# Sliding-window attention in a fused two-layer kernel: norm and softmax work moved between engines, first token tile run to its end first

## The reference, cut to what matters

```python
def mixer_c(h, w_in, q_norm, k_norm, sinks, rel_bias, w_out):
    proj = h @ w_in                                   # 1024 -> 1024 (q) + 256 (k) + 256 (v)
    q, k, v = jnp.split(proj, [SW_HEADS * SW_DIM, (SW_HEADS + SW_KV_HEADS) * SW_DIM], axis=-1)
    q = rmsnorm_2(q.reshape(B, S, SW_HEADS, SW_DIM), q_norm)       # 16 heads of 64
    k = rmsnorm_2(k.reshape(B, S, SW_KV_HEADS, SW_DIM), k_norm)    # 4 heads of 64
    ...
    o = sliding_window_attention(q, k, v, sinks, rel_bias)
    return o.reshape(B, S, C_OUT) @ w_out
# inside, per block of 128 queries against its own and the previous 128 keys:
    logits = jnp.einsum('bqhgd,bkhd->bhgqk', qn, kn) * scale + bias
    m = jnp.maximum(jnp.max(logits, axis=-1, keepdims=True), sink)
    e = jnp.exp(logits - m)
    w = e / (jnp.sum(e, axis=-1, keepdims=True) + jnp.exp(sink - m))
    return jnp.einsum('bhgqk,bkhd->bqhgd', w, vn)
```

## Time and profile before

| | us |
|---|---|
| median of three runs | 1542.4 (1539.7 to 1542.81) |
| span of the profiled execution, first to last instruction | 1536.3 |
| what lies around the span, median less span | 6.1 |
| TensorE busy | 1381.1 |
| VectorE busy | 1029.5 |
| ScalarE busy | 710.5 |
| GpSimd busy | 568.9 |

### The profile page before, as it was taken

How to read it: one execution, slowest core, us unless ns; L and a number is a source line. 1 busy time by engine, 2 the same in 40 slices (tenths; PEclk the granted TensorE clock), 3 DMA queues, 4 the chain that set the end, 5 groups by cost and what they waited for, 6 DMA issues and landing times.

```text
span 1536.3 us, 18265 instructions
## 1 busy us (share of the span) xinstructions
PE 1381.1 (90%) x6001; PEld 969.0 (63%) x6001; DVE 1029.5 (67%) x1917; ACT 710.5 (46%) x1377; POOL 568.9 (37%) x541
## 2 busy tenths in 40 slices
PE   7999998778777887777779999999999999999998
PEld 6887963323333333333336878788888778888887
DVE  4885787666666666666655548659863686498734
ACT  5545453222333332233324463477645655776534
POOL 3040454333333333333344422055433512364414
PEclk9999999998998999999899999999999999999999
DMA  9295699999999999999998510567665443476650
GB/s 315 91 179 189 247 385 422 421 421 422 422 421 422 420 423 422 421 422 422 422 421 312 192 48 13 165 184 203 191 216 194 158 140 92 134 207 195 214 188 28
DMA packets 180739, 414.99 MB, mean 270 GB/s; under 512 B 9178, under 2 KB 113218, under 8 KB 148418
## 3 DMA queue, kind: packets, MB, share of 16 engines
q0 software_dynamic: 37440, 268.45, 42.1%
q1 hardware_dynamic: 143090, 145.66, 30.9%
q10 hardware_dynamic: 144, 0.04, 0.0%
HBM read 409.93 MB, written 4.19 MB: 270 GB/s over the span
## 4 chain that ended last, share of the span: by engine, by line
PE 52%; DMA 23%; DVE 9%; ACT 6%; POOL 5%; issue 4%; ACTq 0%; POOLq 0%; DVEq 0%
DMA expert_rows<-in_peer_uv,route_idx 13%; PE ps L2522 10%; DMA work_b<-in_peer_uv,route_idx 9%; PE ps L2347 8%; PE ps L2063 8%; PE ps L2065 8%; PE ps L2064 8%; PE ps L2523 5%; POOL weights_lo L588 2%; POOL expert_rows L637 2%; ACT weights_hi L433 2%; DVE weights_lo L440 2%; PE ps L2028 1%; DVE expert_rows L1645 1%; POOL ple_proj_lo L588 1%
## 5 line engine op out<-in xcount | busy, mean ns | idle before, releaser
L1645 DVE CUSTOM_DVE_ANT_0 expert_rows<-expert_rows,ps 128x1024 f32<-128x1024 f32 x180 | 219.4, 1220 | 133.9 <-DMA expert_rows<-in_peer_uv,route_idx 132.0
L2347 PE MATMUL ps<-expert_rows,proj 128*128 128x512 f32 x512 | 248.6, 644 | 63.5 <-ACT proj L952 63.5
L637 POOL DMA_INDIRECT expert_rows<-in_peer_uv,route_idx x191 | 184.5, 966 | 288.9 <-PE ps L2347 218.9
L588 POOL TENSOR_TENSOR weights_lo<-weights_raw,weights_hi 128x512 fp32r<-128x512 f32 x116 | 153.4, 1356 | 352.2 <-ACT weights_hi L433 310.3
L433 ACT CAST weights_hi<-weights_raw 128x2048 fp32r<-128x2048 f32 x98 | 185.5, 1917 | 106.3 <-PE ps L2065 82.6
L2347 PEld LDWEIGHTS ps<-expert_rows,proj 128*128 128x128 f32 x512 | 102.9, 206 | 208.4 <-issue 122.5
L2522 PE MATMUL ps<-x_normT,weights_hi 128*128 128x512 f32 x640 | 222.5, 393 | 0.0
L440 DVE TENSOR_TENSOR weights_lo<-weights_raw,weights_hi 128x2048 fp32r<-128x2048 f32 x69 | 163.1, 2370 | 61.2 <-ACT weights_hi L433 60.8
L938 ACT ACTIVATE proj<-proj 128x4 f32<-128x4 f32 x64 | 13.1, 205 | 408.0 <-DVE proj L1645 408.0
L2063 PE MATMUL ps<-weights_hi,x_normT 128*128 128x512 f32 (+1 forms) x496 | 188.2, 379 | 9.3 <-DVE weights_lo L440 3.2
L2065 PE MATMUL ps<-weights_hi,x_normT 128*128 128x512 f32 (+1 forms) x496 | 184.7, 372 | 0.0
(11 more groups left out here) (369 smaller groups left out, 2411.3 us busy)
## 6 DMA issues: line engine op xcount, KB each, us to landing
weights_raw<-in_ffn_up SPq DMA_DIRECT2D x88, 512.0 KB, 5.0
weights_raw<-in_ffn_down SPq DMA_DIRECT2D x22, 1024.0 KB, 5.0
weights_raw<-in_ab_w_in SPq DMA_DIRECT2D x14, 1024.0 KB, 5.1
weights_raw<-in_w_in SPq DMA_DIRECT2D x12, 1024.0 KB, 7.9
weights_raw<-in_ple_gate SPq DMA_DIRECT2D x8, 1024.0 KB, 6.3
weights_raw<-in_c_w_in SPq DMA_DIRECT2D x6, 1024.0 KB, 5.7
weights_raw<-in_w_out SPq DMA_DIRECT2D x4, 1024.0 KB, 12.0
weights_raw<-in_peer_w_query SPq DMA_DIRECT2D x4, 1024.0 KB, 11.9
```

What stands on the lines that cost most here:

```text
L588: ins = pool.tensor_tensor(w.lo[:, c], w.raw[:, c], w.hi[:, c].bitcast(F32), ALU.subtract)
L637: nc.gpsimd.indirect_dma_start(out=dst, out_offset=None, in_=table, in_offset=bass.IndirectOffsetOnAxis(ap=r_idx[:, q, n:n + 1], axis=0)). ...
L1645: ins = nc.vector.tensor_tensor_reduce(out=rows, in0=rows, in1=tokens, scale=1.0, scalar=0.0, op0=ALU.mult, op1=ALU.add, accum_out=r_dot[: ...
L2347: ins = pe.matmul(PS[:, (J[f"peer_{t}"] + m) % 8, :], DIAG[b][:, k, :], rows[:, m * BANK:(m + 1) * BANK], start=False, stop=False, skip_gr ...
```

## The change

1. **Squares on ScalarE.** `square(n, t)` squares a tile of "c" straight from PSUM, with the row scale. VectorE only sums by head.
2. **One eviction with both roots.** VectorE evicts with the row scale and the head's reciprocal root in one operation; the gains of queries and keys are multiplied once and applied to the keys. The last tile (n = 2, t = 1) is the exception: it is evicted first, and squared and scaled in SBUF.
3. **Sums from a ones column.** Each value head gets a 65th column of ones, so the output matmul (65 columns) also gives the softmax sum. A unit's output takes two banks instead of one, and VectorE makes each with an add of the sink, a reciprocal and a product.
4. **First token tile first.** Units are now u = 2t + g. Tile 0's units come first, its output is transposed (`mix2_0`) and its two "cout" tiles run before tile 1's outputs; the residual and the norm of tile 0 (`norm6_0`) come before tile 1's outputs too. `residual_norm` gets `first=False` for this layer. The plan's order is new.
5. **Splits and fillers.** Piece 5 of "c" goes to GpSimd, which no longer waits for steps of the attention ahead of "cout". ScalarE casts "cout" 2 and 3 together behind `mixed_hi(0)`. The calls of `spin` in this stage are gone. `sqrt_table()` is called once more, between the exps of the two tiles.

```diff
-        ("norm5_1", 2), ("c_first", 1), ("c", 3), ("sw_K", 2), ("c_2", 1), ("sw_Q0", 2), ("c_2b", 1),
-        ("sw_L0", 2), ("sw_L1", 4), ("sw_P0", 2), ("sw_O0", 1), ("sw_Q1", 2), ("sw_P1", 4), ("sw_L2", 2), ("sw_L3", 4),
-        ("sw_P2", 2), ("sw_O1", 1), ("sw_P3", 4), ("sw_O2", 1), ("mix2", 2), ("sw_O3", 1), ("mix2b", 2)]
+        ("norm5_1", 2), ("c_00", 1), ("c_01", 1), ("c_10", 1), ("sw_K", 2), ("c_20", 1), ("sw_Q0", 2), ("c_11", 1),
+        ("sw_L0", 2), ("sw_L1", 2), ("c_21", 1), ("sw_P0", 2), ("sw_P1", 2), ("sw_Q1", 2), ("sw_O0", 2), ("sw_O1", 2),
+        ("sw_L2", 4), ("mix2_0", 2), ("sw_L3", 4), ("cout_00", 1), ("sw_P2", 4), ("cout_01", 1), ("sw_P3", 4), ("sw_O2", 2),
+        ("norm6_0", 2), ("sw_O3", 2), ("mix2_1", 2), ("cout_10", 1), ("cout_11", 1), ("norm6_1", 2), ("up1", 2 * FT)]
...
@@ GpSimd
-                    for p in range(0, 4, 2):
+                    for p in (0, 2, 5):
                         split("c", p)
-                    pool.wait_ge(sem("att_max"), TT + 1)
-                    split("cout", 0)
-                    pool.wait_ge(evac_done, END["sw_O0"])
-                    split("cout", 1)
-                    pool.wait_ge(sem("att_max"), TT + 3)
-                    split("cout", 2)
+                    for p in range(3):
+                        split("cout", p)
@@ ScalarE
+            def square(n, t):
+                j = tile_job("c", n, t)
+                dst = window_square(n, t)
+                if (n, t) == (2, 1):
+                    act.wait_ge(evac_done, j + 1)
+                    x = proj_c[:, t, 512:1024]
+                    nc.scalar.activation(dst, x, ACT.Square).then_inc(sem("window_squares"), 1)
+                    return
+                act.wait_ge(pe_done, j + 1)
...
+                nc.scalar.activation(dst, PS[:, j % 8, 0:256 if n == 0 else BANK], ACT.Square,
+                                     scale=root_col(t)).then_inc(sem("window_squares"), 1)
...
             for t in range(TT):
-                window_root(2, t)
-            for p in range(4, 6):
-                split("c", p)
-            for t in range(TT):
+                square(0, t)
                 window_root(0, t)
+                split("c", 4 + t)
+            square(1, 0)
+            window_root(1, 0)
             window_key_pairs(J["sw_K"])
-            window_columns(J["sw_Q0"], 2, QT[:, 0:4])
-            window_root(1, 0)
+            square(2, 0)
+            window_root(2, 0)
+            window_queries(0)
+            square(1, 1)
+            window_root(1, 1)
             for p in halves(0):
                 split("cout", p)
-            window_root(1, 1)
-            exp_unit(0, sink=True)
+            for u in range(2):
+                exp_unit(0, sink=True)
+            square(2, 1)
             weights_out(J["sw_P0"], 0, 0)
+            sqrt_table()
+            window_root(2, 1)
+            weights_out(J["sw_P1"], 0, 1)
+            window_queries(1)
+            mixed_hi(0)
+            for p in halves(1):
+                split("cout", p)
             exp_unit(1, sink=True)
-            window_columns(J["sw_Q1"], 2, QT[:, 4:8])
-            weights_out(J["sw_P1"], 1, 1)
-            split("cout", 2)
-            for u in range(2, SW_UNITS):
-                exp_unit(u % 2, sink=True)
-                weights_out(J[f"sw_P{u}"], u % 2, u)
-            x_hi(J["mix2"], jobs=(0, 1))
-            split("cout", 3)
-            x_hi(J["mix2b"] - 2, jobs=(2, 3))
+            weights_out(J["sw_P2"], 1, 2)
+            exp_unit(1, sink=True)
+            weights_out(J["sw_P3"], 1, 3)
+            sqrt_table()
+            norm_root(6, 0, *(added(tile_job("cout", n, 0)) for n in range(2)))
+            norm_hi(6, 0)
+            mixed_hi(1)
             act_ffn(1, 6, "cout")
@@ VectorE, window_norm(n, t) after its reduce
+                if n == 0:
+                    step(nc.vector.tensor_scalar(V_ONES[:, t, :, 0:HD], src[:, 256:512].rearrange("p (h n) -> p h n", n=HD),
+                                                 root_col(t), None, ALU.mult))
                 reciprocal_root(rs, rs)
...
+                ins = nc.vector.scalar_tensor_tensor(out=d3, in0=s3, scalar=root_col(t), in1=bc(rs, HD), op0=ALU.mult, op1=ALU.mult)
+                freed(ins, j, True)
+                if n == 0:
+                    gain = QK_PRODUCT.unsqueeze(1).unsqueeze(1).broadcast_to([P, SWKV, 2, HD])
+                    step(nc.vector.tensor_tensor(KDUP[:, t], bc(d3, 2), gain, ALU.mult), "keys_ready")
@@ VectorE, order
+            window_norm(0, 0)
             split_lo(v, "c", 3)
+            window_norm(0, 1)
+            split_lo(v, "c", 4)
+            window_norm(1, 0)
+            window_norm(2, 0)
+            window_norm(1, 1)
             v.wait_ge(sem("bias_loaded"), 16)
...
+            window_logits(0)
+            window_logits(1)
+            j = tile_job("c", 2, 1)
+            freed(nc.vector.tensor_scalar(proj_c[:, 1, 512:1024], bank(j), root_col(1), None, ALU.mult), j)
+            window_norm(2, 1)
             window_out(0)
-            window_sums(1)
+            window_out(1)
+            split_lo(v, "cout", 3)
             window_logits(2)
+            mixed_lo(0)
             window_logits(3)
-            window_out(1)
-            window_sums(2)
-            window_sums(3)
+            for n in range(2):
+                v.wait_ge(evac_done, tile_job("cout", n, 0))
+                residual(tile_job("cout", n, 0), 0, n)
+            norm_rstd(0)
             window_out(2)
-            x_lo(J["mix2"], pairs=(0, 1))
+            norm_lo(6, 0)
             window_out(3)
-            split_lo(v, "cout", 3)
-            x_lo(J["mix2b"], pairs=(2, 3))
+            mixed_lo(1)
             vec_ffn(1, 6, "cout")
@@ TensorE, order behind "c" (0, 0) and (0, 1)
+            dense_tile("c", 1, 0)
+            window_keys()
             dense_tile("c", 2, 0)
...
+            dense_tile("c", 1, 1, between=lambda: window_queries(0))
             window_logits(0)
             window_logits(1)
-            spin(J["sw_P0"], 3)
+            dense_tile("c", 2, 1)
             window_T(0)
-            spin(J["sw_O0"], 2)
+            window_T(1)
+            window_queries(1)
             window_out(0)
...
+            window_out(1)
             window_logits(2)
+            window_mixed(0)
             window_logits(3)
-            spin(J["sw_P2"], 3)
+            ready = END["mix2_0"] - 1, END["mix2_0"]
+            dense_tile("cout", 0, 0, ready)
             window_T(2)
-            window_out(1)
-            spin(J["sw_P3"], 2)
+            dense_tile("cout", 1, 0)
             window_T(3)
             window_out(2)
-            window_mixed(0, J["mix2"])
+            norm_T(6, 0)
             window_out(3)
...
+            window_mixed(1)
+            ready = END["mix2_1"] - 1, END["mix2_1"]
+            dense_tile("cout", 0, 1, ready)
+            dense_tile("cout", 1, 1)
+            up_tokens(1, 0, 0)
+            norm_T(6, 1)
+            up_tokens(1, 1, 0)
```

More of the change, by code:

```diff
@@ L897, in mixed, with residual_norm @@
                         split(second, p)
[L899 to L903 removed]
+            def residual_norm(k, name, between, first=True):
+                if first:
+                    sqrt_table()
+                    norm_root(k, 0, *(added(tile_job(name, n, 0)) for n in range(2)))
+                    norm_hi(k, 0)
                 for piece in between:
@@ L2626, in columns_of_tiles @@
-            def columns_of_tiles(c0):
-                return [lambda t, c=c: XN[:, t, c * P:(c + 1) * P] for c in range(c0, c0 + 4)]
-            dense_tile("c", 2, 1, between=lambda: window_queries(0))
+                nk = u // 2 + 1
+                pe.wait_ge(evac_done, END[f"sw_P{u}"])
+                for m in range(2):
+                    b = bank(J[f"sw_O{u}"] + m)
+                    for h in range(4 * m, 4 * m + 4):
+                        o = (h - 4 * m) * (HD + 1)
+                        for k in range(nk):
+                            ins = pe.matmul(b[:, o:o + HD + 1], window_weights(u, h * nk + k)[:, 0, :], V_ONES[:, k, 2 * (u % 2) + m, :],
+                                            start=(k == 0), stop=(k == nk - 1))
+                    ins.then_inc(pe_done, 1)
```

195 lines of the change are left out of this document (100 added, 95 removed).

## The result

The changed kernel takes 1569.0 us (median; 1568.4 to 1570.7) beside 1542.6 for the kernel before on the same chip: slower by 26.4 us. The ratio on record is 1.019 [1.0176, 1.0204]; these two medians alone, of four executions each, give 1.017. Forecast were 1561.0, range 1549 to 1568: the direction is right, the size is short by 8, one microsecond outside the range.

The account below looks back on a forecast made before the run. The prediction took VectorE to set the attention's pace, with TensorE having slack. Queue walk +16.1 us and clock falls +2.5 gave +18.6 on the median 1542.4, so 1561, range 1549 to 1568.

Parts of the forecast that it names:

- What bounds the kernel: Attention: VectorE sets the pace, busy 31.4 of 38.0 us; TensorE has about 10 us to give; the change frees VectorE 16.5.
- Projection: Projection "c": GpSimd's split of piece 5 takes 7.1 us, stops TensorE 3.3 us in the fourth tile, which ends at 1244.9.
- To the second query norm: From the fourth tile's square through ScalarE's casts, table and exp units, ending with VectorE's product at 1268.5.
- First stall: VectorE idles 8 us at the split of "cout" 3, waiting for ScalarE's cast; TensorE idles 7.7 us.
- second tile: After that split, VectorE's logits and low half end at 1290.6; TensorE's logits, transposes and two "cout" tiles end at 1305.1.
- second stall: First norm's reciprocal waits for ScalarE's root until 1312.1, ahead of outputs 2 and 3; last eviction starts 16.1 us later.
- Behind it: From the second norm to the end the order stays and TensorE bounds the stage, so nothing is given back.
- The clock: TensorE's stops of 4.0, 7.7 and 2.7 us lower the granted clock: +1.7 and +0.8 us, at 1.7 a fall.
- the sum 16.1 + 2.5: Whole forecast slowdown: 16.1 us from walking the queues plus 2.5 us for clock falls, 18.6 us.
- A fall at every stop: Rival, chance 0.15: three clock falls under busy TensorE at 1.7 us each, 21.2 us in all, so 1564.
- The clock stays down: Rival, chance 0.08: clock doesn't recover between 1268 and 1332, matmuls cost up to twice, +22 to +50, 1565 to 1592.
- the 6.1: Time taken to lie around the span: the profiled execution's span of 1536.3 against the median of 1542.4 us.

Follow-up runs that it names:

- e4: Changed kernel with GpSimd's three "cout" splits held back until the maxima of unit 1 are made; ratio to the kernel before 1.0168.
- e7: Kernel before, in its order and with its spins, with squares on ScalarE and one eviction taking both roots; ratio 1.0001.
- e1: Changed kernel with 34 spin matmuls put in TensorE's stops; 1558.1 us, ratio to the kernel before 1.0113.
- e10: Like e6, but the low half of piece 5 of "c" is split on VectorE, not GpSimd; 1541.5 us, ratio 1.0014.
- e6: Changed kernel with "cout" casts early, first tile's norm late, GpSimd's "cout" splits held, plus 16 spins; 1546.2 us, ratio 1.0042.
- e9: Kernel before with its four groups of spin matmuls in this stage left out, nothing else; ratio 1.0009.
- e8: Like e7, plus softmax sums from the ones column, still in the order and with the spins of the kernel before; ratio 1.0007.
- e3: Changed kernel with the first tile's norm moved behind the second tile's mixed transposes, its reciprocal behind unit 2's outputs; ratio to the kernel before 1.0129.
- e11: Like e7, with the projection's last tile moved behind the logits, around the first weights' transposes, in place of ten spin records; ratio 1.0007.
- e12: Like e11, plus 14 spin matmuls in the two stops that it leaves; ratio to the kernel before 1.0000.

## Why the prediction was right in direction and short in size

**What bounds the kernel.** Right: VectorE's work was on the path in the attention, and its load fell (12.3 us on the page; the sum said 16.5; with GpSimd held back in e4 the page has 1013.5, 16.0 less than before, so the sum was right and the difference is time held by GpSimd). Unsaid: ScalarE, read as "not far behind", takes VectorE's place at once (e7).

**Projection.** Right but for the clock. GpSimd's split of piece 5 starts at 1235.46 (walked 1235.0), takes 6.88 (7.1), and the stop behind it ends at 1242.39. TensorE stops for 0.96 and 1.79 us there, together 2.75 (walked 3.3). Without a clock fall the fourth tile is squared 27.8 us into the stage (e1), as walked (1244.9 less 1217.2); after, the fall behind the stop adds 1.5 us. The split's own price was not singled out; e10 puts 1.2 us on it.

**To the second query norm.** 1.8 us late at the first exp (1260.44 for 1258.6): 0.4 is the later start of the stage, 1.5 the clock fall in the projection, so the step itself is right up to there. Then it is not unbroken: the second exp unit waits 2.04 us for VectorE's maxima, held by GpSimd. The step let ScalarE run alone and had no term for them. VectorE's product ends the step at 1272.0, walked 1268.5.

**First stall, second tile, second stall.** The mechanism is as walked: both waits stand at the named lines, 9.8 us (8) and 6.04 (6). TensorE's stop ahead of unit 3's logits was to be over 7 us and is 6.17. Removing either wait gives 10 to 11 us, more than the 5.5 worked out for the first: with each goes a stretch of low clock. At full clock the order costs 16.8 us (e1), walked 16.1. That closeness holds some luck: counted from the stage's start e1 reaches the split of "cout" 3 at 66.4 us, walked 64.8, and the reciprocal of the norm at 95.0, walked 94.9. So the walk was 1.5 us early at the first and made up for it at the second.

**Behind it.** Right: 220.3 and 220.2 us.

**The clock. This is the step that failed.** It is the term of +2.5 in the sum 16.1 + 2.5: a fall at 1.7 us (half of 3.3), times one and a half, from the earlier trace rows. e1 measures 13.9 in its place. Two things were off. The count: the clock fell four times, at each of the three stops named and once in the projection. And the length, which weighs more: the stretches last 3, 17, 7 and 17 us. The fall in the projection, ahead of 512-column products as in the expert stage of the earlier trace rows, lasted 3.4 us and cost 1.5, about as priced. Those of 17 us come where TensorE does transposes, 65-column outputs and logits, with pauses of its own; why the clock stays low there, no run shows. And the loss is not only on TensorE's own work: its lateness lengthens VectorE's wait by 2.1 us. Two rivals had a part each. "A fall at every stop" (0.15) had the number of falls behind the query transposes, at a price far too small. "The clock stays down" (0.08) had the long stretches and from +22 the right size, though it described one stretch to 1332, and the clock recovered twice before that. It deserved more than its chance. The Trainium skill (TensorE: Matmul & The Clock Gate, "Why this matters for your kernels") advises against gaps of some microseconds between bursts of matmuls, and e1 and e6 agree; e9 shows a case where two falls cost 1.7 us together.

**The accounts, by the stage.** +30.7 = 13.9 clock (after to e1: 12.4 at the stops of the attention and the norm, 1.5 in the projection) + 13.2 the three edits of order at full clock (e1 to e6) + 1.2 piece 5 (e6 to e10) + 2.5 open (e10 to before). e1 and e6 have different numbers of spins, so the first two can trade about a microsecond. The port (e4) has no share of its own in it that can be measured. The time's +26.4 is less than +30.7 because of what it is counted from. What lies around the span is 1.8 us in the changed kernel (1569.3 less 1567.5) and in the profiled executions of the experiments. With the same 1.8 the execution profiled before took 1538.1 (an estimate), 4.5 below the median of 1542.6, and the later medians of that kernel are 1539.2 to 1539.7. So the 6.1 that the prediction took to lie around the span was mostly the scatter of three executions, and 1542.4 was about 3 us too high a start. From one profiled execution to the other the forecast of 18.6 stands against 31.2: the miss in the mechanism is 12.6 us, and the high start hid 4 to 5 of it.

## What to carry to other kernels

When a reorder opens stops in TensorE's queue, price the clock by what runs behind the stop, not only by its length: a fall in front of transposes and narrow matmuls lasted 17 us and cost 6.6 us at once and 4.3 at the end of the stage, one in front of 512-column products lasted 3 and cost 1.5. Before moving work off the busiest engine, look at who releases the step behind it if that engine were done at once: here ScalarE's casts and table load stood there already, and 8 to 10 us less on VectorE gave nothing that can be measured. In queues kept in order, look for a wait placed ahead of ready work; two such places cost some 20 of 31 us, their share of the clock included. And before a small difference between two traces is believed, compare them up to the edit: 1.5 of e4's 1.6 us lay ahead of it.

## What the runs showed of the hardware that was not expected

**One program, one stop, with and without a clock fall.** The stop at GpSimd's split (1.8 us) is followed by 3 us of low clock in three of seven executions of the same code. e7 and e8 stop 2.65 us each ahead of the first weights' transposes; in e7 they run at full clock (1.09 us, shown under e7), in e8 not:

```profile
1268.39 1.96 PE L2053 MATMUL ps<-consts,work_a 128*128 128x128 f32 x8 [2.65 <-ACT work_a L872]
```

So the length of a stop alone did not decide it here, and one trace of a kernel shows one outcome.

**A weight split of two lengths.** The same VectorE weight split, at the same place of the program, takes 3.1 us in twelve of the fourteen profiled executions and 6.8 in two (e8, e10). VectorE and GpSimd in e7, and then in e8:

```profile
1191.67 3.10 DVE L447 TENSOR_TENSOR weights_lo<-weights_raw,weights_hi 128x2048 fp32r<-128x2048 f32 x1 [0.40 <-ACT weights_hi L440]
```

```profile
1191.31 7.11 POOL L595 TENSOR_TENSOR ple_proj_lo<-ple_proj_raw,ple_proj_hi 128x512 fp32r<-128x512 f32 x4
```

```profile
1193.44 6.82 DVE L449 TENSOR_TENSOR weights_lo<-weights_raw,weights_hi 128x2048 fp32r<-128x2048 f32 x1 [0.39 <-ACT weights_hi L442]
```

```profile
1193.09 5.03 POOL L597 TENSOR_TENSOR ple_proj_lo<-ple_proj_raw,ple_proj_hi 128x512 fp32r<-128x512 f32 x4
```

Either GpSimd's four parts make room for VectorE (7.1 and 3.1) or they run through (5.0) and VectorE ends 2.1 us behind the last of them (6.8), about the 2.29 that such a split takes alone. In e8 and e10 this falls on the path and their stages start 5.7 and 6.4 us later than before's; in e1 the same happened in the last gate, and its tail is 223.1 us in place of 220.3. In e3, e11 and e12 the stage starts 3 to 5 us late without it. In these three, and in no other trace, the granted clock is at 0.50 for 10 us from about 964 on (windows of e11, then of e7):

```profile
964.00:968.00 4.00, 4.00 (x17) 2.34 (x17) 2.82 (x3) 0.01 (x1) 0.00 (x0) 0.50 1.06 378
```

```profile
964.00:968.00 4.00, 4.00 (x33) 2.90 (x34) 3.93 (x5) 0.69 (x2) 0.00 (x0) 1.00 1.09 358
```

The way from the stop ahead of it to the next weights is 18.5 us in all three and 15.6 before and in e7: 2.9 us of the late start. This scatter is why the stage was read from the traces.
